# State-space mixer of a hybrid backbone: exponents broadcast by DMA, outputs feature-major, gate under the out product

## The reference, cut to what matters

```python
def ssd_scan(x, dt, A, Bm, Cm, h0):              # chunks of 128 tokens
    def step(h, inp):
        xc, dtc, Bc, Cc = inp
        cum = jnp.cumsum(dtc * A, axis=1)
        seg = jnp.where(causal, cum[:, :, None] - cum[:, None], -jnp.inf)
        wts = jnp.einsum('bign,bjgn->bijg', Cc, Bc)[..., None] * jnp.exp(seg) * dtc[:, None]
        y = jnp.einsum('bijgr,bjgrp->bigrp', wts, xc)
        y = y + jnp.einsum('bign,bgrpn->bigrp', Cc, h) * jnp.exp(cum)[..., None]
        w_end = jnp.exp(cum[:, -1:] - cum) * dtc
        h = h * jnp.exp(cum[:, -1])[..., None, None] + jnp.einsum('bjgn,bjgr,bjgrp->bgrpn', Bc, w_end, xc)
        return h, y
...
    xbc = jax.nn.silu(dwconv_same(xbc, conv_w, conv_b))      # 3 taps, 1536 features: x, B, C
    dt = softplus(dt_raw + dt_bias)
    y = y_f + flip(y_b) + d_skip * xs                         # scans of both directions, and the skip
    y = rmsnorm(y * jax.nn.silu(z), norm_g)                   # the gate
    ms = jnp.concatenate([y_na, y_ssd], axis=-1) @ w_out_even # the out product
```

## Time and profile before

| | us |
|---|---|
| median of 3 runs | 3571.57 (3570.52 to 3580.82) |
| the profiled execution | 3568.97 |
| its span, first to last instruction | 3567.2 |
| PE busy | 3305.9 (93%) |
| DVE busy | 2008.8 (56%) |
| ACT busy | 922.7 (26%) |
| POOL busy | 583.9 (16%) |

### The profile page before, as it was taken

How to read it: one execution, slowest core, us unless ns; L and a number is a source line. 1 busy time by engine, 2 the same in 40 slices (tenths; PEclk the granted TensorE clock), 3 DMA queues, 4 the chain that set the end, 5 groups by cost and what they waited for, 6 DMA issues and landing times. The chain is left out here.

```text
span 3567.2 us, 46417 instructions
## 1 busy us (share of the span) xinstructions
PE 3305.9 (93%) x17976; PEld 2861.9 (80%) x17976; DVE 2008.8 (56%) x3402; ACT 922.7 (26%) x1783; POOL 583.9 (16%) x547
## 2 busy tenths in 40 slices
PE   4899998987968999999999979999988999999997
PEld 3565554554547999999999968888888999999996
DVE  4896551237975755445554567665456544555446
ACT  2212442121234421211122143222243122111211
POOL 0010100007751211111011002322232111101110
PEclk9999999998988999999999999999999999999999
DMA  5562101000024411111111022222142111111111
GB/s 206 206 274 82 26 22 56 24 0 24 1 88 123 127 42 36 47 41 44 44 36 47 24 81 64 68 65 64 38 146 77 36 48 47 41 41 35 47 41 59
DMA packets 164382, 233.52 MB, mean 65 GB/s; under 512 B 17260, under 2 KB 138772, under 8 KB 159884
## 3 DMA queue, kind: packets, MB, share of 16 engines
q1 hardware_dynamic: 164236, 231.53, 19.5%
HBM read 214.86 MB, written 16.63 MB: 65 GB/s over the span
## 5 line engine op out<-in xcount | busy, mean ns | idle before, releaser
L1574 PE MATMUL PS<-AHL,WH 128*128 128x384 f32 x3072 | 780.8, 335 | 6.0 <-DVE WL L1842 6.0
L1574 PE MATMUL PS<-Y,WH 128*128 128x384 f32 x3072 | 780.1, 334 | 3.1 <-issue 3.1
L1862 DVE SCALAR_TENSOR_TENSOR XT<-PS,MOD,XT 128x384 f32<-128x384 f32 (+2 forms) x1024 | 495.3, 514 | 222.1 <-PE PS L1574 222.0
L1574 PEld LDWEIGHTS PS<-AHL,WH 128*128 128x128 f32 x3072 | 555.5, 188 | 6.6 <-DVE WL L1842 6.6
L1574 PEld LDWEIGHTS PS<-Y,WH 128*128 128x128 f32 x3072 | 554.5, 188 | 4.2 <-issue 3.7
L1574 PE MATMUL PS<-AHL,WL 128*128 128x384 f32 x1536 | 513.6, 334 | 0.0
L1574 PE MATMUL PS<-Y,WL 128*128 128x384 f32 x1536 | 513.1, 334 | 0.0
L1849 DVE TENSOR_TENSOR AHL<-SQ,AHL 128x384 fp32r<-128x384 f32 x192 | 156.9, 817 | 431.9 <-ACT AHL L1675 431.9
L1776 POOL TENSOR_TENSOR SQ<-RT 128x384 f32<-128x384 f32 x192 | 180.1, 938 | 1319.3 <-ACT RT L1670 1299.9
L537 PE MATMUL PS<-HT,WR 128*128 128x384 f32 x960 | 319.0, 492 | 26.3 <-PEq L437 15.5
L1664 ACT ACTIVATE WH<-WU 128x1024 fp32r<-128x1024 f32 x128 | 135.6, 1059 | 728.6 <-DMA WU<-in_wff 728.6
(11 more groups left out here) (329 smaller groups left out, 4427.6 us busy)
## 6 DMA issues: line engine op xcount, KB each, us to landing
WU<-in_wff SPq DMA_DIRECT2D x128, 512.0 KB, 3.5
XT<-in_wmod SPq DMA_DIRECT2D x13, 2048.0 KB, 10.6
F<-in_wmod SPq DMA_DIRECT2D x9, 2048.0 KB, 9.6
OWR<-in_wslots SPq DMA_DIRECT2D x24, 768.0 KB, 4.9
WR<-in_wslots SPq DMA_DIRECT2D x8, 2048.0 KB, 8.0
PW<-in_wslots SPq DMA_DIRECT2D x24, 512.0 KB, 4.6
OWOR<-in_wslots SPq DMA_DIRECT2D x24, 512.0 KB, 4.3
EX<-b_rows SPq DMA_DIRECT2D x72, 128.0 KB, 3.1
```

What stands on the lines that cost most here:

```text
L1574: mm = nc.tensor.matmul(out, wt(w), x, start=(n == 0 and i == 0), stop=(n == len(terms) - 1 and i == 2))
L1862: ins = nc.vector.scalar_tensor_tensor(out=x, in0=PS[:, 3 + j % 4, a - c * TC:e - c * TC], scalar=MOD[:, l, 40 + b, cond:cond + 1], in1=x, ...
```

## The change

Nothing of what is computed changes. Outside the mixer the program is the same.

- Z is computed feature-major, 24 tiles of 128 features x 384 tokens, and stored in 8 stores of 576 KB. The attention's output is stored in DRAM too (`yna_spill`), and the first weights of the convolution are loaded during attention.
- The convolution runs its blocks in the order 8 to 11, 0 to 7. Step sizes, decay sums, the rows of the cumulated decays, and the products under masks (`GB`) are made between its blocks, and the preparation stage is gone. The skip term is made by ACT, one block at a time, and stored. The cumulated decays are stored in two orders (34 DMAs). The transposes have two PSUM banks instead of three (the banks 4 and 7 serve the preparation).
- The scan reads its exponents by DMA: 1 MB a step for the decays between tokens, spread over all partitions, and two DMAs of 256 KB for the state's part. POOL masks 12 heads, DVE the other 4, ACT takes the exponential head by head with a bias. y is feature-major. The context's states get a place of their own.
- The gate stage is gone. Z, y and the attention's part are gated, scaled and split by chunk of 384 tokens inside the out product's block: chunk 0 ahead of the first tile, the chunks 1 and 2 between tiles 0 to 7 and 8 to 15. PE sums the squares of a chunk before tiles 0, 4 and 12.

The core of the diff (names and waits as in the new kernel):

```diff
@@ convolution, PE
-                            j = 3 * n + c
-                            if j >= 3:
-                                pe.wait_ge(turned_taken.sem, turned_taken.at(j - 2))
-                                mm = nc.tensor.transpose(PS[:, 5 + j % 3, t * P:(t + 1) * P],
+                        j = 3 * n + c
+                        if j >= 2:
+                            pe.wait_ge(turned_taken.sem, turned_taken.at(j - 1))
+                            mm = nc.tensor.transpose(PS[:, 5 + j % 2, t * P:(t + 1) * P], turn_source(i, 3 * c + t), ident)
@@ convolution, PE: behind the products of block i
+                    if i >= 1 and (i - 1) in turns:
+                        turn(i - 1)
+                    prep(i)
@@ convolution, ACT: in silu(i)
+                    if b < 8:
+                        if b >= 1:
+                            act.wait_ge(skip_stored.sem, skip_stored.at(16 * b))
+                        act.activation(DX[:, 0:CTX], src[0], ACT.Copy, scale=DCOL[:, b:b + 1]).then_inc(act_own.sem, act_own.one())
+                        act.activation(DX[:, CTX:T], src[1], ACT.Copy, scale=DCOL[:, b:b + 1]).then_inc(act_own.sem, act_own.one())
@@ scan, SP
+                def rows_in(n):
+                    if n >= 4:
+                        sp.wait_ge(chunk_summed.sem, chunk_summed.at(n - 3))
+                    sp.dma_start(EXS[n % 4][:, :, :], cum_rows[n % 2, n // 2, :, :].unsqueeze(0).broadcast_to((P, SH, P)))\
...
+                for n in range(3):
+                    pairs_in(n)
+                for d in range(2):
+                    sp.dma_start(HS[:, d, :], ssd0[:, d, :]).then_inc(state_in[d].sem, 16)
+                rows_in(2)
+                rows_in(3)
+                for c in range(NC):
+                    sp.dma_start(YL[c][:, :, :], skip_spill.rearrange("b p t -> p b t")[:, :, c * TC:(c + 1) * TC])\
@@ scan, POOL
-                    nc.gpsimd.tensor_tensor(RW[:, n % 2, :, :], DTA[:, t, hs].unsqueeze(2).broadcast_to((P, SH, P)),
-                    nc.gpsimd.tensor_tensor(xdt[:, n % 2, :, :], x,
-                    nc.gpsimd.tensor_tensor(xw[:, n % 2, :, :], x, WEND[:, t, hs].unsqueeze(2).broadcast_to((P, SH, SP)),
+                for n in range(NS):
+                    if n + 1 < NS:
+                        carry(n + 1)
+                    if n + 2 < NS:
+                        masked(n + 2)
+                        inputs(n + 2)
@@ scan, PE
+                for n in range(NS):
+                    if n + 1 < NS:
+                        read(n + 1)
+                        update(n + 1)
+                    chunk(n)
@@ out product, PE
+                        if l == 0 and n in (4, 12):
+                            gate_sum(n // 8 + 1)
@@ out product, ACT, in the loop over n, behind the weight tile
+                        if l == 0 and c < 2:
+                            if b < 4:
+                                (gate_silu if b < 2 else gate_square)(c + 1, b % 2)
+                                attn_split(c + 1, b)
@@ out product, POOL
+                    def gate_tree(c):
+                        pool.wait_ge(square_sum_ready.sem, 2 * c + 2)
+                        for m, w in enumerate((4, 2, 1)):
+                            if m:
+                                pool.wait_ge(gate_squares_added.sem, gate_squares_added.at(3 * (c - 1) + m))
+                            nc.gpsimd.tensor_tensor(ZH[c][:, 0:w, :], ZH[c][:, 0:w, :], ZH[c][:, w:2 * w, :], ALU.add)\
+                              .then_inc(gate_squares_added.sem, 1)
```

More of the change, by code:

```diff
@@ new lines, in softplus_act @@
+        def softplus_act(act, x, s, part):
+            a, e, u, l = (s[:, n, :] for n in range(4))
+            act.wait_ge(softplus_dve_part.sem, softplus_dve_part.at(part))
+            if part == 1:
+                act.activation(a, x, ACT.Abs).then_inc(act_own.sem, act_own.one())
+                act.wait_ge(act_own.sem, act_own.n)
+                act.activation(e, a, ACT.Exp, scale=-1.0).then_inc(softplus_act_part.sem, 1)
+            else:
+                act.activation(l, u, ACT.Ln).then_inc(softplus_act_part.sem, 1)
@@ new lines, in _ @@
+                nc.vector.memset(ZROW[0:1, 0:512].bitcast(F32), 0.0).then_inc(half_masked.sem, 1)
+                masked(0)
+                inter(0)
+                masked(1)
+                weights(0)
+                add_state(0)
+                for n in range(NS):
+                    if n + 1 < NS:
+                        if n >= 1:
+                            dve.wait_ge(step_taken.sem, step_taken.at((n - 1) // 2))
+                        inter(n + 1)
+                    if n % 2 == 0 and n >= 2:
+                        output(n // 2 - 1, n + 2 if n + 1 < NS else NS)
+                    if n + 2 < NS:
+                        masked(n + 2)
@@ L1756, in _ @@
                             split_low(0, k)
+                    else:
+                        for k in range(4):
+                            attn_rest(0, k)
+                        for b in range(1, KD, 2):
+                            gate_rest(0, b)
                     for n in range(NW):
@@ L1760, in _ @@
                             split_low(c + 1, b)
+                        if l == 0 and c < 2:
+                            if b < 4:
+                                attn_rest(c + 1, b)
+                            if b == 3:
+                                gate_tree(c + 1)
+                            for m in {5: range(0, 2), 6: range(2, 5), 7: range(5, 8)}.get(b, ()):
+                                gate_rest(c + 1, m)
                         if b >= 1:
@@ L1899, in _ @@
                         out_unit(n)
+                    if l == 0:
+                        gate_mean(0)
+                        for b in range(KD):
+                            gate_scale(0, b)
+                            if b % 2 == 1 and b >= 3:
+                                gate_low(b - 3)
+                        gate_low(6)
                     for n in range(NW):
@@ L1934, in out_and_mlp @@
             if l == 0:
-                xback.close(16)
+                for c in range(NC):
+                    x_in[c].close(16)
+                mix_high.close(NC * KD)
+                mix_low.close(4)
+                mix_low_pool.close(20)
+                gate_squares_added.close(6)
+                gate_summed.close(3)
             for n in range(NB):
```

1066 lines of the change are left out of this document (629 added, 437 removed).

## The result

The changed kernel takes 3629.37 us (median of 4 runs, 3624.06 to 3635.90), the kernel before 3571.94 in the same comparison: ratio 1.0161, 95% interval 1.0137 to 1.0185. It is slower by 57 us, where the prediction had 3578 and its range ended at 3613.

The account below looks back on a forecast made before the run. It took PE, busy 93% of the run, and in the scan the SBUF lock between DVE and POOL as bounds. Terms -4 + 25 + 8 - 9 - 15 - 23 + 24 = +6 on 3568.97 gave 3575, as median 3578; range 3548 to 3613.

Parts of the forecast that it names:

- Ahead of the convolution: Before the first features: weights now come during attention, so the convolution starts 4 us earlier, -4 (0 to -8).
- Convolution loop: Twelve convolution blocks: waits for copies plus work moved in from preparation, 256 us against 231, +25 (+18 to +28).
- clock: Convolution: nine repeated pairs of PE gaps each cost half of 1.5 us at the lower clock level, +8 (0 to +16).
- preparation: Between the convolution's last eviction and the scan's start: some 12.5 us remain of 21.3, -9 (-4 to -12).
- third group waits behind the taps: Convolution: with two banks, PE's third transposes wait for DVE's copy behind the next block's taps, 2.5 us in nine blocks, +23.
- Scan: Scan stage: steady step 11.3 us against 11.9, whole scan 215 against 230.1, -15 (-26 to -4).
- the shared sum is the bound: Scan: DVE's and POOL's SBUF work excludes each other, so a step costs their sum, 10.7 us, taken as 11.3.
- rival B: Scan and convolution: PE falls to the low clock and its step exceeds 11.3 us, +27 and +8, 3613; chance 0.20.
- D: Scan: the exponents' DMA is slower than large loads, a step becomes 12.8 us, +24, 3602; chance 0.05.
- Gate ahead of tile 0: From the scan's end to the first out tile's end: only chunk 0 gated, 36 us against 59.3, -23 (-17 to -28).
- Gate under the tiles: Out tiles: PE's sums wait 9 and 10 us for POOL's tree, plus two returns from low clock, +24 (+8 to +30).
- The second term of 10: Out tiles: eight tiles after tile 4, PE's sum waits again for POOL's tree, 10 us.

Follow-up runs that it names:

- c_three_banks: The changed kernel with three PSUM banks for the transposes again, features get three instead of four, copies still behind the taps: 3597.08 us, ratio 1.0074.
- c_silu_early: The changed kernel with DVE's copies ahead of the taps and ACT's SiLU ahead of the last eviction in the convolution: 3576.06 us, ratio 1.0016.
- s_mask8: The changed kernel with POOL masking 8 heads and DVE 8 in the scan, instead of 12 and 4: 3626.07 us, ratio 1.0162.
- s_scale_dve: The changed kernel with DVE, not POOL, scaling the state in the scan, directly ahead of the state's update: 3625.80 us, ratio 1.0161.
- o_pe_sum: The changed kernel with PE adding up the squares of chunks 1 and 2 itself, POOL's additions gone: 3614.32 us, ratio 1.0124.
- o_root_early: The changed kernel with root, first scalings, splits and rests of chunks 1 and 2 one tile earlier in the engines' lists: 3609.44 us, ratio 1.0113.

## Why the prediction was wrong

**Ahead of the convolution, -8.3 for -4.** Right in kind, at the end of its bounds.

**Convolution loop, clock and preparation, +32.7 for +24.** The step "third group waits behind the taps" is right in mechanism, and in size where it stands alone (2.30 us where I had 2.5, in six of nine blocks); in all it was 15.6 us for 22.5. That PE's idle time in the loop came out near the forecast all the same (18.6 us more) is luck: the 7 us more for the SiLU, which I did not have, filled the gap. The term that failed is the clock: I halved the loss of the old row of 779 and took 8 for nine blocks (nine halves of 1.5 are even 6.8). c_three_banks shows 18.7. My upper bound of 16 was too low as well. A second term was too small. The loop, from the first features to the end of the last, took 273.4 us where I had 264 with the clock term, against 230.9 before. Besides the idle time that is 24 us more of busy PE. By c_three_banks (busy 225.7 us at a clock of 0.97) and c_silu_early (222.3 at 0.99), against 241.8 after and 217.9 before, 16 to 20 of them are clock and 4 to 8 the work moved into the loop, where I had let all but 2 us of it vanish inside waits. Preparation came out as worked out, 11.5 us for 12.5.

**Scan, -0.6 for -15.** The step that failed is "the shared sum is the bound", in two ways. One price was wrong: I scaled POOL's masking from the 3.60 us of the old L1209 by the number of heads, 2.70; it takes 3.42 alone and 4.42 beside DVE. The old operation reads one operand spread over 128 elements, the new one reads a full one. With it, and DVE's masking at 0.68, the sum is 11.5 and not 10.7. And the sum itself isn't a law: s_mask8 lowers it by half a us, s_scale_dve by 0.7, and both gain nothing. What the step costs, 12.0 us for 11.3, is by the rows DVE's list plus what POOL blocks of it; sixteen steps make 11 of the 14 us, the start and end of the scan the rest. The first third of y was there 21.6 us after the scan's start (843.62 to 865.17), inside the 17 to 27 that I had, and below the 24 to 34 that it would be with 6.9 us more for the loads of 64 partitions. Of rival B the low clock came about (0.75 in the mean, PE busy 147 of 229 us), but not its condition, a mean under 0.58: PE waited 53.3 of 160 us for DVE's update of the state, so PE's own work was not the bound. D was not either: in the changed kernel ACT waits for its exponents' DMA for 5.7 of 160 us.

**Gate ahead of tile 0, -20.1 for -23.** Near in total, 38.5 us where I had 36, but with luck in one term: PE's sum of the squares took 8.0 us for 4, by the same wrong pace as in o_pe_sum, while the SiLUs, products and squares ahead of it took 5.9 for 8.

**Gate under the tiles, +52.2 for +24.** The largest miss. The wait for the tree was priced at 19 and measured 22.2. The second term of 10 was for the tree again, ahead of tile 12, and in between I took PE to be free. I had listed what stands ahead of PE's sum, but not what stands ahead of its next user: root, scalings and rests for tile 8, behind a weight tile that waits for PE. That is 15.0 us. Again the clock: some 12 us where I had 4. o_root_early removes the wait of 15.0 with the work of all engines unchanged, so it was order alone.

In sum, of the 53 us that the forecast missed in the profile, 28 are in the tiles, 14 in the scan, 4 up to the end of the preparation (more clock loss and more work in the loop, less an earlier start), 3 in the gate and 3 in the unchanged rest. The clock accounts for some 8 in the tiles and 11 in the convolution, the unseen wait for 15. I had put the large clock losses into one rival, B. They needed no bound on PE: they came in the convolution and in the tiles, behind the pauses that the change adds.

## What to carry to other kernels

- Price a pause of PE twice: once for its length, and once for the slower matmuls behind it. In the convolution the second was as large as the first (18.7 and 15.6 us), in the tiles a third of it (12 and 39 us).
- When work is slid under a loop, follow each product to its last consumer, and for every step of it ask what stands ahead in the same engine's list and what that waits for. A wait for a DMA that itself waits for the engine you feed is a bad neighbour: here it held the root back by 13 us.
- Before giving up a buffer or bank, look at what its release stands behind. Moving the release (DVE's copies) ahead of the long work gave back 22 of the 32 us that the bank itself gave back.

## What the runs showed of the hardware

- POOL's elementwise operations did not cost by elements alone: 1.76 ns an element per partition with one spread operand and a constant (3.60 us for 2048), 1.86 with one full and one spread (1.90 for 1024), 2.23 for the masking in place with full rows (3.42 for 1536). Size is not the reason: in s_mask8 the masking has 1024 elements and takes 2.34 us. Nor is writing in place, since the scaling of the state does that in 1.90. That it is the kind of operands fits and was not tested by itself.
- Short pauses of PE that repeat cost clock: one of 1.75 us in a block left the features at 15.65 us, a second of 2.30 us close behind it made them 16.80 (c_three_banks and the changed kernel). It was not the same everywhere: behind pauses of 3.20 and 0.85 us with the small products after them, the features took 15.75.
- DVE and POOL blocked each other in both directions and for whole instructions. DVE's masking of four heads took 3.9 us beside POOL's and 0.68 us alone, and POOL's took 4.4 us beside DVE's addition to y and 3.42 us alone. POOL waits until the addition has ended at 980.28, and DVE's masking until POOL's has ended at 983.56:

```profile
978.56 1.72 DVE L1530 TENSOR_TENSOR yl<-yl,EB 128x1024 f32<-128x1024 f32 x1
979.15 4.41 POOL L1409 TENSOR_TENSOR EXS<-EXS,CO 128x1536 f32<-128x1536 f32 x1
980.20 3.92 DVE L1515 TENSOR_TENSOR EXS<-EXS,CO 128x512 f32<-128x512 f32 x1
```
